# Interleaved high and low weight words, and bulk products that run from the last column to the first

## What is computed

```
h = rms_norm(x); proj = h @ w_in                      # 1024 x 3080, then delta rule, pooling, convolutions
x = x + mixed @ w_out                                 # 1024 x 1024
ff = silu(h @ w_gate) * (h @ w_up); x = x + ff @ w_down    # 1024 x 2816, twice, and back
x = rms_norm(x + sigmoid(x @ ple_gate) * (p @ ple_proj))
mix = token_mixer(rmsnorm(x) @ w_in_2)                # mLSTM and latent attention
x = x + rmsnorm(mix @ w_out_2)
x = x + rmsnorm(square(relu(m @ w_up_2)) @ w_down_2)  # 1024 x 4096 and back
```

## Time and profile before

| what | value |
|---|---|
| median of 3 runs | 1336.55 us (1336.36 to 1343.49) |
| profiled execution | 1336.49 us, its span from first to last instruction 1334.5 us |
| mean granted TensorE clock over the span | 0.988 |
| PE busy | 1284.3 us, 96% |
| PEld busy | 1020.2 us, 76% |
| DVE, ACT, POOL busy | 588.5, 507.0, 568.5 us |
| DMA | 113.39 MB, mean 85 GB/s |

### The profile page before, as it was taken

How to read it: one execution, slowest core, us unless ns; L and a number is a source line. 1 busy time by engine, 2 the same in 40 slices (tenths; PEclk the granted TensorE clock), 3 DMA queues, 4 the chain that set the end, 5 groups by cost and what they waited for, 6 DMA issues and landing times.

```text
span 1334.5 us, 15423 instructions
## 1 busy us (share of the span) xinstructions
PE 1284.3 (96%) x6025; PEld 1020.2 (76%) x6025; DVE 588.5 (44%) x840; ACT 507.0 (38%) x782; POOL 568.5 (43%) x430
## 2 busy tenths in 40 slices
PE   7989999999999999999999998799899999999997
PEld 5768887878888888888878755465688888888886
DVE  4998344341154211112576345465486414325124
ACT  5575325352222222212544334554354323223132
POOL 4333532545555545544644331301355444545440
PEclk9999999999999999999999999999999999999998
DMA  6422321333333333323422321101223333333321
GB/s 178 151 63 48 79 66 50 109 87 111 95 95 95 101 103 96 96 83 98 103 79 65 94 48 48 47 17 32 79 77 103 98 101 96 96 96 95 96 62 64
DMA packets 216303, 113.39 MB, mean 85 GB/s; under 512 B 21588, under 2 KB 214304, under 8 KB 215976
## 3 DMA queue, kind: packets, MB, share of 16 engines
q1 hardware_dynamic: 215128, 109.45, 29.0%
q10 hardware_dynamic: 976, 2.90, 0.6%
q0 software_dynamic: 128, 0.07, 0.0%
HBM read 110.03 MB, written 2.38 MB: 84 GB/s over the span
## 4 chain that ended last, share of the span: by engine, by line
PE 80%; DVE 5%; ACT 3%; POOL 1%; issue 1%; DMA 0%; SPq 0%; DVEq 0%; ACTq 0%
PE bank L1996 22%; PE bank L1998 21%; PE bank L1997 21%; PE bank L1143 1%; PE aux L1159 1%; PE aux L1072 1%; PE bank L1021 1%; PE aux L1996 1%; PE bank L1023 1%; PE bank L1022 1%; PE aux L1084 1%; PE bank L2044 1%; POOL wl L1950 1%; PE bank L2046 1%; PE bank L2045 1%
## 5 line engine op out<-in xcount | busy, mean ns | idle before, releaser
L1950 POOL TENSOR_TENSOR wl<-raw,wh 128x512 fp32r<-128x512 f32 (+1 forms) x402 | 545.3, 1379 | 703.7 <-ACT wh L2374 703.6
L2374 ACT CAST wh<-raw 128x1024 fp32r<-128x1024 f32 (+1 forms) x201 | 208.3, 1039 | 384.0 <-PE bank L1998 362.0
L1996 PE MATMUL bank<-ah,wh 128*128 128x512 f32 x888 | 352.0, 396 | 0.4 <-DVE craw L2770 0.4
L1998 PE MATMUL bank<-al,wh 128*128 128x512 f32 x888 | 345.9, 390 | 0.0
L1997 PE MATMUL bank<-ah,wl 128*128 128x512 f32 x888 | 345.8, 389 | 0.0
L1996 PEld LDWEIGHTS bank<-ah,wh 128*128 128x128 f32 x888 | 166.9, 188 | 40.1 <-issue 6.0
L1997 PEld LDWEIGHTS bank<-ah,wl 128*128 128x128 f32 x888 | 166.8, 188 | 34.9 <-issue 1.2
L1998 PEld LDWEIGHTS bank<-al,wh 128*128 128x128 f32 x888 | 166.7, 188 | 35.1
L1996 PE MATMUL bank<-yh,wh 128*128 128x512 f32 x488 | 190.6, 391 | 0.1
L1998 PE MATMUL bank<-yl,wh 128*128 128x512 f32 x488 | 190.0, 389 | 0.0
L1997 PE MATMUL bank<-yh,wl 128*128 128x512 f32 x488 | 189.9, 389 | 0.0
(11 more groups left out here) (451 smaller groups left out, 1549.5 us busy)
## 6 DMA issues: line engine op xcount, KB each, us to landing
raw<-in_w_up SPq DMA_DIRECT2D x54, 512.0 KB, 3.9
raw<-in_w_down SPq DMA_DIRECT2D x48, 512.0 KB, 3.9
raw<-in_w_in SPq DMA_DIRECT2D x39, 512.0 KB, 3.9
raw<-in_w_gate SPq DMA_DIRECT2D x22, 512.0 KB, 3.8
raw<-in_w_out SPq DMA_DIRECT2D x16, 512.0 KB, 3.6
raw<-in_ple_gate SPq DMA_DIRECT2D x8, 512.0 KB, 3.9
raw<-in_w_down SPq DMA_DIRECT2D x8, 384.0 KB, 3.3
xtok<-in_x SPq DMA_DIRECT2D x4, 512.0 KB, 5.3
```

What stands on the lines that cost most here:

```text
L1950: nc.gpsimd.tensor_tensor(wl[pl.slot[b]][:, half], raw[b % RAW][:, half], wh[pl.slot[b]][:, half].bitcast(F32), ALU.subtract).then_inc(wl_ ...
L1996: nc.tensor.matmul(ps, h[:, c:c + P], mh[:, k, :], start=(n == 0), stop=False)
L1998: last = nc.tensor.matmul(ps, h[:, c:c + P], ml[:, k, :], start=False, stop=(n == nk - 1))
L2374: nc.scalar.copy(wh[pl.slot[b]][:, 0:w], raw[b % RAW][:, 0:w]).then_inc(wh_ready, 1)
```

## The change

Two things are changed, and nothing else in the program: every engine has the same instructions in the same order with the same waits.

First, `wh` and `wl` of a slot become one tile of 2048 words, `parted`. In it word 0 is the first high word, word 1 the first low word, and so on: a high or a low part is every second word of the tile, a step of 8 bytes. ACT's cast writes with this step, POOL's subtraction reads `wh` and writes `wl` with it, and the weight loads read with it. The five blocks whose weights serve as moving operand (`moved(b)`: the `ukv` block and the 256 wide blocks of `w_in_2`) are left in two contiguous halves. The total size and the place of the buffers after them stay as they were.

Second, the bulk products with the weights as stationary operand take moving operand and bank through `backward`: 512 (or 256) columns from the last to the first. Every column still meets its own place in the bank. Products on lines 1021 to 1023, and all others that are not made of high and low parts, stay as they were.

```
+def backward(columns):
+    return columns[:, ::-1]
...
-        wh = [sb(f"wh{i}", [P, WB], F32R) for i in range(SPLIT)]
-        wl = [sb(f"wl{i}", [P, WB], F32R) for i in range(SPLIT)]
+        parted = [sb(f"wh{i}", [P, 2 * WB], F32R) for i in range(SPLIT)]
...
+        def moved(b):
+            what = pl.blocks[b]
+            return what[0] == "ukv" or what[:2] == ("mat", "w_in_2") and what[5] == 256
+
+        def part_of(b, part):
+            w = parted[pl.slot[b]]
+            if moved(b):
+                return w[:, part * WB:(part + 1) * WB]
+            return w[:, :].rearrange("p (n two) -> p n two", two=2)[:, :, part]
...
-                    nc.gpsimd.tensor_tensor(wl[pl.slot[b]][:, half], raw[b % RAW][:, half],
-                                            wh[pl.slot[b]][:, half].bitcast(F32), ALU.subtract).then_inc(wl_ready, 1)
+                    nc.gpsimd.tensor_tensor(wl(b)[:, half], raw[b % RAW][:, half],
+                                            wh(b)[:, half].bitcast(F32), ALU.subtract).then_inc(wl_ready, 1)
...
-                    nc.tensor.matmul(ps, h[:, c:c + P], mh[:, k, :], start=(n == 0), stop=False)
-                    nc.tensor.matmul(ps, l[:, c:c + P], mh[:, k, :], start=False, stop=False)
-                    last = nc.tensor.matmul(ps, h[:, c:c + P], ml[:, k, :], start=False, stop=(n == nk - 1))
+                    nc.tensor.matmul(backward(ps), h[:, c:c + P], backward(mh[:, k, :]), start=(n == 0), stop=False)
+                    nc.tensor.matmul(backward(ps), l[:, c:c + P], backward(mh[:, k, :]), start=False, stop=False)
+                    last = nc.tensor.matmul(backward(ps), h[:, c:c + P], backward(ml[:, k, :]), start=False, stop=(n == nk - 1))
...
-                    nc.scalar.copy(wh[pl.slot[b]][:, 0:w], raw[b % RAW][:, 0:w]).then_inc(wh_ready, 1)
+                    nc.scalar.copy(wh(b)[:, 0:w], raw[b % RAW][:, 0:w]).then_inc(wh_ready, 1)
```

More of the change, by code:

```diff
@@ L1255, in last_half @@
                     c = slice(k * stride + col, k * stride + col + P)
-                    nc.tensor.matmul(ps, h[:, c], mh[:, k, s], start=(k == 0), stop=False)
-                    nc.tensor.matmul(ps, l[:, c], mh[:, k, s], start=False, stop=False)
-                    last = nc.tensor.matmul(ps, h[:, c], ml[:, k, s], start=False, stop=(k == nk - 1))
+                    nc.tensor.matmul(backward(ps), h[:, c], backward(mh[:, k, s]), start=(k == 0), stop=False)
+                    nc.tensor.matmul(backward(ps), l[:, c], backward(mh[:, k, s]), start=False, stop=False)
+                    last = nc.tensor.matmul(backward(ps), h[:, c], backward(ml[:, k, s]), start=False, stop=(k == nk - 1))
                     if between and k == nk - 2:
@@ L2016, in gemm_triple @@
                         ps = bank[u % NBANK][:, :]
-                        nc.tensor.matmul(ps, wh[pl.slot[b]][:, c], ah[:, k, :], start=(k == 0), stop=False)
-                        nc.tensor.matmul(ps, wl[pl.slot[b]][:, c], ah[:, k, :], start=False, stop=False)
+                        nc.tensor.matmul(backward(ps), wh(b)[:, c], backward(ah[:, k, :]), start=(k == 0), stop=False)
+                        nc.tensor.matmul(backward(ps), wl(b)[:, c], backward(ah[:, k, :]), start=False, stop=False)
                     pe.wait_ge(al_ready, KD * fill + k + 1)
@@ L2021, in gemm_triple @@
                         b = pl.tiles[u][2]
-                        last = nc.tensor.matmul(bank[u % NBANK][:, :], wh[pl.slot[b]][:, c], al[:, k, :], start=False,
+                        last = nc.tensor.matmul(backward(bank[u % NBANK][:, :]), wh(b)[:, c], backward(al[:, k, :]), start=False,
                                                 stop=(k == KD - 1))
@@ L2043, in gemm_pair @@
                         ps = bank[u % NBANK][:, :]
-                        nc.tensor.matmul(ps, wh[pl.slot[b]][:, c], ah[:, k, :], start=(n == 0), stop=False)
-                        nc.tensor.matmul(ps, wl[pl.slot[b]][:, c], ah[:, k, :], start=False, stop=False)
-                        last = nc.tensor.matmul(ps, wh[pl.slot[b]][:, c], al[:, k, :], start=False, stop=(n == KD - 1))
+                        nc.tensor.matmul(backward(ps), wh(b)[:, c], backward(ah[:, k, :]), start=(n == 0), stop=False)
+                        nc.tensor.matmul(backward(ps), wl(b)[:, c], backward(ah[:, k, :]), start=False, stop=False)
+                        last = nc.tensor.matmul(backward(ps), wh(b)[:, c], backward(al[:, k, :]), start=False, stop=(n == KD - 1))
                         if n == KD - 1:
@@ L2109, in first_pair @@
                     c = slice(k * P, k * P + P)
-                    nc.tensor.matmul(bank[u][:, :], wh[u][:, c], zh[:, k, :], start=(k == 0), stop=False)
-                    nc.tensor.matmul(bank[u][:, :], wh[u][:, c], zl[:, k, :], start=False, stop=False)
+                    nc.tensor.matmul(backward(bank[u][:, :]), wh(u)[:, c], backward(zh[:, k, :]), start=(k == 0), stop=False)
+                    nc.tensor.matmul(backward(bank[u][:, :]), wh(u)[:, c], backward(zl[:, k, :]), start=False, stop=False)
                     for j in low.get(k, ()):
                         c = slice(j * P, j * P + P)
-                        last = nc.tensor.matmul(bank[u][:, :], wl[u][:, c], zh[:, j, :], start=False,
+                        last = nc.tensor.matmul(backward(bank[u][:, :]), wl(u)[:, c], backward(zh[:, j, :]), start=False,
                                                 stop=(j == KD - 1))
```

13 lines of the change are left out of this document (8 added, 5 removed).

## The result

| | before | after |
|---|---|---|
| median | 1336.85 us (4 runs, 1336.36 to 1343.49) | 1370.55 us (4 runs, 1366.80 to 1378.39) |
| ratio | | 1.022, 95% interval 1.019 to 1.025 |
| profiled execution (span) | 1336.49 (1334.5) us | 1378.39 (1376.4) us |
| granted clock, mean | 0.988 | 0.986 |
| PE busy | 1284.3 us, 96% | 1327.0 us, 96% |

The change makes the kernel slower: the medians lie 33.7 us apart, and the ratio amounts to 30 us. The forecast was 1297 us, range 1284 to 1346; it was wrong in sign. The profiled execution of the changed kernel happens to be the longest of its four, 8 us above their median, so its trace shows more loss than the medians do.

What follows compares the result with a forecast made beforehand. PE, busy for 96% of the span, was taken to bound the kernel, with about 893 us of bulk products on the path. 1336.5 us - 41.4 (shorter products) + 2 (cast and subtraction) = 1297 us, range 1284 to 1346.

Steps and rivals of the forecast that it cites:

- the excess over the columns: Bulk products of 512 columns: 226.7 ns apart against 213.3 ns for their columns, so 13.4 ns each, within TensorE's own traffic.
- The number of products on the path, 3,940: Bulk products of 512 columns on the path: 893 us divided by 0.2267 us each.
- with one pace the two streams either never meet or step apart once: SBUF reads of bulk products: weight load and moving operand both at 8 bytes per 0.8 ns, regaining 10.5 ns per product.
- The term of 41.4 us: Bulk products on the path: 3,940 products each 10.5 ns shorter, 41.4 us less.
- The direction: Bulk products taken last to first: sets the relative direction of load and moving reads, assumed to run together; no separate size.
- Rival D: Bulk products: a load spanning 1024 bytes doubles the meetings, excess 26.8 ns, product 240 ns, 1392 us; chance 0.07.
- Rival E: Bulk products: backward reading or writing falls to full float32 pace, 429.6 ns per product, 2138 us; chance 0.09.
- Rival B: Bulk products: only half of the 10.5 ns is regained, 221 ns per product, 1318 us; chance 0.10.
- Rival C: Bulk products: the 13.4 ns are a constant that neither step nor direction moves, 1338 us; chance 0.14.
- The cast and the subtraction: ACT's cast and POOL's subtraction at a step of 8 bytes: 10% longer, 2 us more on the path.
- Rival F: POOL becomes the slower station if a strided subtraction exceeds 2.59 us; doubled, 1367 us; chance 0.04.
- The 256 column products: 48 products at the end: 109 to 110 ns apart instead of 120.0, 0.5 us less, counted at nothing.

## Why the prediction was wrong

*What bounds the kernel, and where the excess lies: right.* PE's bulk products set the time before and after, the excess over the columns is real and not a constant of the product kind (216.9 ns with a still operand), it lies in TensorE's own reads of SBUF, and it is the same for 384 and 512 columns. The number of products on the path, 3,940, is in the right range: 3,800 from the still operand, and the operand read backward gives 25.8 us for 6.6 ns, 3,900; the medians of backward alone (22.7 us for 6.7 ns) and of the shifted kernel before (16.7 us for 5.8 ns) give 3,400 and 2,900. No other engine took over.

*The step that failed* is "with one pace the two streams either never meet or step apart once", and with it the choice of the value. Interleaving makes the load walk as many bytes as the operand in the same time, and instead of giving 10.5 ns back it costs 6.7 per product read forward at the start 0; of the seven combinations of direction and start that were tried none came below 230.1 ns. The term of 41.4 us was thus a gain that no run shows; what stood in its place was a loss of 6.7 to 10 ns per product. I had one reading for two distances in one row, and one for a small excess at half the operand's pace, and made a rule of movement out of them that neither row contained. The earlier trace rows doesn't even speak of places, since its two distances come from the same tiles behind a break in the row. The still load shows the mistake: with a load that doesn't walk at all, the excess is 18 ns, not less.

The reading of the earlier trace rows was weak too. The products of 256 columns stand about 120 ns apart in the kernel before and in the changed one, so what holds them there doesn't react to the change, and their 13.3 ns needn't be the excess of the longer products.

*The direction* I had called the weakest step, for not knowing which way the load walks. It fails more simply: backward costs 6.7 ns with contiguous weights too, in the operand alone. Which way a load walks stays unknown.

*Rival D* (slower, from 53 us for a doubled excess) had the sign and the place: the distance in a row above 226.7 ns. Its size was too big, 13.4 ns where the interleaving costs 6.7 and the whole change 10 at most; at 10 ns its sum would have been 3,940 x 10 = 39 us and 1378 us, which is the longest execution and 7 us above the median. Its reason fell as well: at a start of 128 bytes the wider load costs nothing (231.3 against 232.6 ns), so the sign was right by another cause. I gave it 0.07. That it was the only rival in which the added bytes of a load cost anything, and that no row of the trace had a step other than one word, were reasons to give it as much as the forecast.

*Rival E* (backward falls to half pace) fell: 233.4 and not 430 ns. The Trainium skill (PSUM — Partial Sum Buffer, Specifications) says that any access pattern that is not contiguous slows products significantly; here neither a reversed bank nor a bank in pairs changed the count of 566, so for these two orders the measurement goes against a strict reading of the sentence.

*Rival B* (half of the gain, 221 ns) was met by no run. *Rival C* (nothing can change) fell too. Beside the constancy of the excess it had for it the rule of the Trainium skill (TensorE: Matmul & The Clock Gate, Part 2) that loading the next weights takes nothing from the running product. That the same program with its weight tiles 128 bytes further on takes 232.6 instead of 226.8 ns says otherwise, at least for these operands.

*The cast and the subtraction* were sized well enough: 10% forecast for both, 11% and 0.4% measured. With 6 casts on the path, 0.12 us each, that is under 1 us where I had 2. *Rival F* needed 2.59 us of POOL and met 1.39.

*The 256 column products* at the end: in the profile after, 119 ns from start to start (rows below: 10 steps in 1.19 us) and 120 before, where I had 109 to 110. They neither gained nor lost; why was not tried.

```profile
1358.98 0.28 PE L1280 MATMUL bank<-yh,wh 128*128 128x256 f32 x1
...
1360.17 0.28 PE L1281 MATMUL bank<-yl,wh 128*128 128x256 f32 x1
```

**What stays open.** How the reads of the two streams disturb each other isn't settled. Known is that the distance depends on the start of the weight tiles, on whether the operand walks, on its direction and, at one start, on the step of the load; that the excess is the same for 384 and 512 columns; and that it doesn't fall with a still load (231.3) or one of half the length (229.7). Known is also that one kernel can hold two distances (233.3 and 236.7) and changes between them at breaks in the row. A load's start rather than its length, or an order in which SBUF is read that the profile doesn't show, would fit; neither was tested. No run leaves the load out, and none repeats a trace of the changed kernel, so how much of the excess the load makes, and how often 236.7 ns come about, stays open too.

## What to carry to other kernels

When a row of products stands a constant few per cent above its columns, hold one operand still in a throwaway kernel before any change is built: that run gives an upper bound of what can be won (10 ns here, of which no correct kernel won any) and says which stream it belongs to. Addresses of tiles are part of a tuned kernel: moving them by 128 bytes cost 1.3%, and an edit that changes a tile's layout should be compared at several starts, and each variant at the same start as its counterpart. One window of one execution is not the kernel: compare several stretches, and the times of all executions with the one that was traced. A mechanism read from two rows is a guess on a third case; where the edit enters a form of access that no row has, give the rival that it costs something as much weight as the forecast.

## What the runs showed of the hardware that I had not expected

- The distance between bulk products takes the values 226.8, 230.1, 231.3, 232.6, 233.4 and 236.9 ns with nothing changed but addresses, steps and direction of what is read, at a granted clock of 1.00 throughout.
- Within one execution of one kernel the same kind of product holds one of two distances for up to hundreds of us and changes over at breaks in the row: 233.3 and 236.7 ns in the changed kernel, 230.1 and 233.0 in the forward one at 64 bytes.
- A bank may be written backward or in pairs 256 bytes apart at no cost (566 products in 128 us in both cases), while the same backward order costs 6.7 ns when it is read from SBUF, and pairs in both together cost 259 ns.
- A moving operand that is one column 512 times is read at full pace: 216.9 ns.
- ACT's cast of 1024 words to a step of 8 bytes takes 7 to 11% longer (1115 to 1155 ns in the interleaved kernels, 1039 before), POOL's subtraction from and to that step 0 to 1.3% (1384 to 1397 ns, 1379 before).
